# Two blocks with expert layers on one core: new heads for the expert stages, and the third down matrix loaded in mixer 2

## The reference

```
g_idx = argmax(group logits);  e_logits = expert logits of that group
top_v, top_i = top_k(e_logits, 2);  gate = softmax(top_v) * softmax(group logits)[g_idx]
out = sum over the token's 2 experts:  gate * ((silu(x @ w1[e]) * (x @ w3[e])) @ w2[e])
```

## Time and profile before

| | |
|---|---|
| median of 3 runs | 1572.54 us (1571.43 to 1575.5) |
| profiled execution, span from first to last instruction | 1574.9 us (no time outside the span is shown) |
| mean granted clock of TensorE | 0.939 of full speed |
| busy: PE, DVE, ACT, POOL | 1353.3, 689.2, 247.8, 80.0 us |
| moved by DMA | 528.20 MB, mean 335 GB/s |
| first expert stage begins | 167.5 us |
| second expert stage begins | 1124.2 us |

### The profile page before, as it was taken

One profiled execution on the slowest core, in us unless ns is written; L12 is line 12 of the kernel. 1 busy time (PEld: TensorE's weight loads), 2 busy tenths in 40 slices (PEclk: granted clock), 3 DMA queues, 4 the chain that ended last, 5 costly groups with the idle time before them and its releaser, 6 DMA issues. The chain is left out here.

```text
span 1574.9 us, 27743 instructions
## 1 busy us (share of the span) xinstructions
PE 1353.3 (86%) x11912; PEld 876.2 (56%) x11912; DVE 689.2 (44%) x1844; ACT 247.8 (16%) x505; POOL 80.0 (5%) x125
## 2 busy tenths in 40 slices
PE   9999998997978789899999999999896676666665
PEld 8655554553455566588767748886453343333332
DVE  4634664322223343427687536652562332332333
ACT  2322330110001111233223113230200000000000
POOL 2401000000000000030000200100000000000000
PEclk9999999999988999999999999999998878887887
DMA  9965899999999999877522454476999999999996
GB/s 336 270 232 191 335 426 429 424 425 427 427 430 425 426 425 427 352 251 280 200 93 106 148 174 160 165 284 257 381 393 429 429 430 429 431 430 430 430 427 252
DMA packets 94023, 528.20 MB, mean 335 GB/s; under 512 B 8282, under 2 KB 10610, under 8 KB 67684
## 3 DMA queue, kind: packets, MB, share of 16 engines
q1 hardware_dynamic: 88792, 521.30, 81.8%
q0 software_dynamic: 2624, 5.32, 1.4%
q10 hardware_dynamic: 2508, 0.17, 0.1%
HBM read 525.70 MB, written 1.07 MB: 334 GB/s over the span
## 5 line engine op out<-in xcount | busy, mean ns | idle before, releaser
L1568 PE MATMUL ps<-weight_ring,e_xT 128*32 128x256 f32 x3456 | 247.8, 449 | 131.4 <-DMA weight_ring<-in_w_up_dram 89.2
L1568 PEld LDWEIGHTS ps<-weight_ring,e_xT 128*32 128x32 f32 x3456 | 137.0, 128 | 237.6 <-issue 192.7
L1848 DVE TENSOR_TENSOR e_g<-e_act_g,ps 128x128 f32<-128x128 f32 x64 | 24.8, 388 | 263.5 <-ACT e_act_g L1655 262.3
L1846 DVE TENSOR_TENSOR e_act_g<-e_act_g,ps 128x128 f32<-128x128 f32 x32 | 9.2, 286 | 236.2 <-ACT e_act_g L1655 236.2
L1655 ACT ACTIVATE e_act_g<-ps 128x128 f32<-128x128 f32 x64 | 17.8, 278 | 565.5 <-PE ps L1568 558.3
L1568 PE MATMUL ps<-expert_set,e_xT 128*32 128x256 f32 x640 | 51.3, 491 | 42.5 <-DMA expert_set<-in_w_up_dram 42.5
L1598 PE MATMUL ps<-weight_ring,e_gT 128*32 128x256 f32 x1344 | 82.6, 387 | 4.2 <-DVE e_gT L1852 2.0
L2369 PE MATMUL ps<-expert_set,weight_ring 128*128 128x256 f32 x384 | 84.2, 379 | 0.0
L2369 PEld LDWEIGHTS ps<-expert_set,weight_ring 128*128 128x128 f32 x384 | 73.0, 190 | 9.9
L1532 PE MATMUL ps<-e_y,e_routing 32*128 32x256 f32 x1024 | 74.3, 404 | 2.1 <-DVE e_y L1880 1.5
L1524 PE MATMUL ps<-e_n,e_Gt 128*32 128x256 f32 x1056 | 70.9, 385 | 3.8 <-DVE e_Gt L1795 2.0
(11 more groups left out here) (614 smaller groups left out, 1945.4 us busy)
## 6 DMA issues: line engine op xcount, KB each, us to landing
weight_ring<-in_expert_w_dram SPq DMA_DIRECT2D x80, 2048.0 KB, 23.0
weight_ring<-in_w_in_dram SPq DMA_DIRECT2D x26, 2048.0 KB, 9.6
weight_ring<-in_w_down_dram SPq DMA_DIRECT2D x20, 2048.0 KB, 38.8
weight_ring<-in_w_gate_dram SPq DMA_DIRECT2D x19, 2048.0 KB, 32.9
weight_ring<-in_w_up_dram SPq DMA_DIRECT2D x19, 2048.0 KB, 37.4
weight_ring<-in_w_ada_dram SPq DMA_DIRECT2D x12, 2048.0 KB, 12.6
expert_set<-in_w_gate_dram SPq DMA_DIRECT2D x10, 2048.0 KB, 33.4
expert_set<-in_w_up_dram SPq DMA_DIRECT2D x10, 2048.0 KB, 37.9
```

Source lines behind the costliest of these rows:

```text
L1568: mm = pe.matmul(ps[32 * j:32 * j + 32, 4, 0:256].rearrange("p (w f) -> p w f", w=2), xT[:, k, :], w13[:, :, k, j * P:(j + 1) * P], start= ...
L1848: dve.tensor_tensor(g[:], spread(act_g[:]), spread(ps[:, 4, P:2 * P]), ALU.mult).then_inc(s_g, 1)
```

## The change

In `moe`:

- Expert 0 gets a direct mask: a token takes it if group 0 holds the group maximum and the expert's logit reaches the second highest of the group's eight. Two small position matmuls (`first_positions`) and a one-hot come from that alone. The full choice follows, while PE gathers expert 0 and does its up.
- The full position matmuls (`positions`) stand in the middle of expert 0's up, the one-hots of experts 1 and 2 come straight from positions and choices, and slots, gates and `wide` are worked out in DVE's part of expert 0.
- PE transposes `wide` in expert 1, behind its gather and in front of its combine (then behind expert 0's down). In stage 1 the residual stands behind expert 1's up (then expert 0's).
- The counts of `keep_busy` are others, and in stage 2 the residual is split around the first steps.
- In stage 2 a down is now queued behind an earlier expert's pair (`DOWN_AFTER`), and `load_down(2)` is no longer in the head.

In `mixer2`: the transposed `h` goes where `yT` was, the router's buffers (`spare`) to the end of `FT`, the squares' junk to `misc`; the third down of stage 2 is loaded behind piece 22 (the first of branch b).

The order of the downs:

```diff
-        DOWN_AFTER.update((i, i) for i in range(11 if SETS == 2 else 5, STATIC))
+        DOWN_AFTER.update(((i, i) for i in range(11, STATIC)) if SETS == 2 else
+                          ((i, {3: 6, 5: 5}.get(i, i + 1)) for i in range(3, STATIC - 1) if i != 4))
...
-            for i in (2, 4) if last else (3,):
+            for i in (4,) if last else (3,):
                 load_down(i)
```

PE, the head (`positions` holds the four matmuls of L1516 to L1519, `first_positions` two for expert 0):

```diff
+            def first_positions():
+                pe.wait_ge(s_hot0, 1)
+                pe.wait_ge(s_iota, 1)
+                pe.matmul(pos0_ps, tri[:], hot0, start=True, stop=False, skip_group_check=True)
+                pe.matmul(pos0_ps[:, 1:2], c.ones[:], hot0[:, 0:1], start=False, stop=True, skip_group_check=True).then_inc(s_pos0, 1)
+            def positions():
+                pe.wait_ge(s_hot, 1)
...
             if x is not None:
                 x.pe_transposes(pe)
-                keep_busy(c, pe, 7, 11)
+                keep_busy(c, pe, 7, 2)
             else:
-                residual()
-                keep_busy(c, pe, 7, 4)
+                residual((0, 1))
+            first_positions()
+            if x is not None:
+                keep_busy(c, pe, 7, 6)
+            else:
+                residual((2,))
             pe.wait_ge(s_n, 2)
             pe.wait_ge(s_Gt, 1)
             gather()
-            keep_busy(c, pe, 7, 4)
+            if x is not None:
+                keep_busy(c, pe, 7, 8)
+            else:
+                residual((3,))
+                keep_busy(c, pe, 7, 3)
```

PE, `expert(i)`, behind the first half of the up and behind its end:

```diff
                     if known and i == 0 and k == KD // 2 - 1:
                         mm.then_inc(s_uph, 1)
+                        positions()
...
-                if first:
-                    if x is not None:
-                        x.pe_taken(pe)
-                        residual()
-                elif x is not None and known:
+                if x is not None and second:
+                    x.pe_taken(pe)
+                    residual()
+                if x is not None and known and not first:
                     x.pe_early(pe, i)
                 pe.wait_ge(s_Gt, i + 2)
                 pe.wait_ge(s_y, i + 1)
                 gather()
+                if second:
+                    pe.wait_ge(s_slot, 1)
+                    for v in range(8):
+                        mm = pe.transpose(ps[:, 6 + v // 4, (v % 4) * P:(v % 4 + 1) * P], wide[:, v, :], c.ident[:])
+                    mm.then_inc(s_rows, 1)
                 if not first:
-                    pe.wait_ge(s_Gw, i + 1)
+                    pe.wait_ge(s_Gw, i)
                     combine()
```

DVE, the head; left out are the group index and mask and the best two, as before but with `take_x(0)` among them, the copy of the positions, the one-hot of expert 1 and the block counts:

```diff
             link(dve.tensor_reduce(gm[:], gl, AX_X, ALU.max))
+            for tt in range(TT):
+                ins = dve.max(top8[:, tt, :], el[:, tt, 0:EPG])
+            link(ins)
+            link(dve.tensor_tensor(slot[:, 1, :], el[:, :, 0], top8[:, :, 1], ALU.is_ge))
+            link(dve.tensor_tensor(hot0, gl[:, :, 0], gm[:], ALU.is_ge))
+            dve.tensor_tensor(hot0, hot0, slot[:, 1, :], ALU.mult).then_inc(s_hot0, 1)
...
+            dve.wait_ge(s_pos0, 1)
+            link(dve.tensor_copy(pos0, pos0_ps))
+            for tt in range(TT):
+                ins = dve.tensor_scalar(Gt[:, tt, :], ie[:], pos0[:, tt:tt + 1], hot0[:, tt:tt + 1], ALU.is_equal, ALU.mult)
+            ins.then_inc(s_Gt, 1)
```

DVE, expert 0 behind its product, `take_x(1)` and the gather of block 1; then `GwT` as before:

```diff
                 dve.wait_ge(s_gather, i + 2)
+                begin = isinstance(i, int) and i == 0
+                if begin:
+                    early_one_hot(2)
+                    slots_and_gates()
+                    gated_y()
                     rows()
+                    step(VO - 4, dve.tensor_scalar(slot[:], slot[:], -2.0 * SLOTS, None, ALU.add))
```

`mixer2`, the buffers, SP's loads and ACT's squares:

```diff
-        hT, spare = nT, nTp[:].rearrange("p k n -> p (k n)")
+        hT, spare = yT, FT[:, 4128:4128 + 2048]
...
-        junk = FT[:, 4128:4128 + 2048]
+        junk = [misc[:, 512 * g:512 * g + 512] for g in range(3)] + [FT[:, 2080:2592]]
...
             for p in M2_ISSUE:
                 sp.wait_ge(*used(M2_BEFORE[p]))
                 m2_load(c, sp, t, p)
+                if p == 22:
+                    sp.wait_ge(s_fl, 16)
+                    load_one(c, sp, c.s_e2, 2, 2, W, third=c.three)
...
             for g in range(3):
                 act.wait_ge(s_h, g + 1)
+                if g == 2:
+                    act.wait_ge(s_arow, 48)
                 squares(g)
```

More of the change, by code:

```diff
@@ L1344, in moe @@
         slot = sb("slot", [P, 2, TT])
+        hot0, pos0 = slot[:, 0, :], gate[:, 1, :]
         over = etmp
@@ L1500, in _, with residual @@
         def _(pe):
-            def residual():
-                for m in range(4):
+            def residual(ms=range(4)):
+                for m in ms:
                     mm = pe.matmul(ps[:, m, :].rearrange("p (t n) -> p t n", t=TT), c.ident[:], h[:, :, m * 256:(m + 1) * 256],
                               start=True, stop=False, skip_group_check=True)
-                mm.then_inc(s_comb, 1)
-            if x is not None:
-                x.pe_transposes(pe)
-                keep_busy(c, pe, 7, 11)
-            else:
-                residual()
-                keep_busy(c, pe, 7, 4)
[L1514 to L1519, removed]
+                if ms[-1] == 3:
+                    mm.then_inc(s_comb, 1)
+            def first_positions():
[5 more added lines that the diff above has]
+                pe.wait_ge(s_hot, 1)
+                pe.matmul(pos_ps, tri[:], both[:].rearrange("p t e -> p (t e)"), start=True, stop=False, skip_group_check=True)
+                pe.matmul(pos_ps[:, NE:2 * NE], c.ones[:], both[:, 0, :], start=False, stop=True, skip_group_check=True).then_inc(s_pos, 1)
+                pe.matmul(tot_ps, c.ones[:], both[:, 0, :], start=True, stop=False, skip_group_check=True)
+                pe.matmul(tot_ps, c.ones[:], both[:, 1, :], start=False, stop=True, skip_group_check=True).then_inc(s_tot, 1)
             def gather():
@@ L1600, in expert @@
                 mm.then_inc(s_down, 1)
[L1601 to L1605, removed]
                 if x is not None and second:
@@ L1749, in _ @@
             link(ins)
+            dve.wait_ge(s_Gt, 1)
+            dve.tensor_tensor(gate[:, 0, :], top8[:, :, 1], top8[:, :, 0], ALU.subtract).then_inc(s_vd, 1)
             below(etmp, em, lambda tt: top8[:, tt, 0:1], NE)
             link(below(pos, em, lambda tt: top8[:, tt, 1:2], NE))
+            take_x(0)
             link(dve.tensor_reduce(topi[:], etmp[:], AX_X, ALU.min))
@@ L1798, in _ @@
-            dve.wait_ge(s_ve, 1)
-            link(dve.tensor_scalar(gate[:, 0, :], gate[:, 1, :], 1.0, None, ALU.add))
-            link(dve.tensor_tensor(gate[:, 0, :], gate[:, 0, :], gprob[:], ALU.mult))
-            link(dve.reciprocal(gate[:, 0, :], gate[:, 0, :]))
-            link(dve.tensor_tensor(gate[:, 1, :], gate[:, 0, :], gate[:, 1, :], ALU.mult))
-            if last:
-                dve.wait_ge(s_comb, 1)
-                dve.wait_ge(s_n, 2)
-            for v in range(8):
-                src = (slot, gate)[v // 4][:, (v // 2) % 2, v % 2:v % 2 + 1]
-                ins = dve.tensor_copy(wide[:, v, :], src.to_broadcast([P, P]))
@@ L1877, in expert @@
                     block_table()
-                if mod is not None:
-                    dve.wait_ge(s_down, i + 1)
-                    dve.tensor_tensor(y[:], ps[:, 5, 0:256], gate_m[:], ALU.mult).then_inc(s_y, 1)
+                if not begin:
+                    gated_y()
             if mod is not None:
@@ L2088, in _ @@
         def _(sp):
+            W = [t[x] for x in ("w_gate_2", "w_up_2", "w_down_2")]
             for p in M2_ISSUE:
@@ L2601, in squares @@
                 at = 2 * tile + half
-                act.activation(junk[:, g * 512:g * 512 + 512], h[:, tile, half * 512:half * 512 + 512], ACT.Square,
+                act.activation(junk[g], h[:, tile, half * 512:half * 512 + 512], ACT.Square,
                                accum_out=stat[:, 0, at:at + 1]).then_inc(s_hsq, 1)
```

104 lines of the change are left out of this document (54 added, 50 removed).

## The result

The changed kernel takes 1580.07 us (median of 8 runs, 1578.08 to 1582.44); beside it, on the same chip, the kernel before took 1575.5 (8 runs, 1571.43 to 1576.65). The ratio is 1.0034 with a 95% interval of 1.0024 to 1.0044: some 5.4 us slower (0.0034 x 1575.5). The forecast was 1571.8 with 1577.3 as its upper end; it stood on 1572.54, the median of three runs of the kernel before, where the eight give 1575.5.

The account below looks back on a forecast made before the run. SP's weight stream was taken to bound the expert stages and PE's chain mixer 2. First head +3.5, mixer 2's tail +1.7 and second head -5.9 gave -0.7 us on 1572.54: 1571.8, range 1566.3 to 1577.3.

Parts of the forecast that it names:

- What bounds the kernel: SP's weight stream bounds both expert stages, so time lost at a head stays; in mixer 2 PE's chain counts.
- A: First expert stage's head: the chain through expert 1 delays weight loads, costing +3.5 us.
- E4: Load of expert 4's gate and up pair; first-stage issue forecast at 209.8, second-stage at 1142.4.
- E5: Load of expert 5's gate and up pair; first-stage issue forecast at 224.1, second-stage at 1156.3.
- clock rival: PE's pause before combine 1 lowers its clock in both heads: first head +6.9, second -2.8, total 1578.3; chance 0.17.
- The two rows: Old-profile idle windows for judging the clock: 259 to 262, then clock 0.57; 1537 to 1541, clock kept at 1.00.
- the forecast pause of 3.75 us: First head: PE idles in front of combine 1, from 192.8 to 196.55, while DVE copies rows and builds weights.
- B: Mixer 2's tail: the early third down delays the last modulation piece by 4.9 us, costing +1.7 us.
- C: Second expert stage's head: earlier up 0 and one down fewer there, gaining 5.9 us.
- What I costed at nothing: Mixer 2's moved transposed h, router buffers and squares' junk, and the third square's added wait: 0 us.
- The sum and its range: +3.5 + 1.7 - 5.9 = -0.7 us, giving 1571.8; range 1566.3 to 1577.3 to hold 8 in 10.
- its base: Starting time 1572.54 us, the old kernel's median, taken though the profiled span was 1574.9.

Follow-up runs that it names:

- experiment 3: Changed kernel with the first expert stage as in the kernel before; 1575.79 us, ratio 1.0005 to the kernel before.
- experiment 4: Changed kernel with the old first expert stage and the third down issued behind mixer 2's last modulation piece; 1570.40 us, ratio 0.9972 to the kernel before.
- experiment 5: Kernel before with only the changed first expert stage put in; 1580.93 us, ratio 1.0038 to the kernel before.
- experiment 11: Changed kernel, first stage's residual behind the transposes, third down loaded at the second stage's head, none in mixer 2; 1574.80 us, ratio 0.9997.
- experiment 2: Changed kernel with the third down issued behind mixer 2's last modulation piece instead of in front; 1575.96 us, ratio 0.9997 to the kernel before.
- experiment 7: Changed kernel with the first stage's residual behind the transposes, in front of combine 1; 1572.93 us, ratio 0.9990 to the kernel before.
- 1: Changed kernel with 14 filler matmuls in the first stage's pause in front of combine 1; 1577.00 us, ratio 1.0011 to the kernel before.
- experiment 8: Changed kernel with the edits of experiment 2 and experiment 7 together; 1570.91 us, ratio 0.9967 to the kernel before.
- experiments 9: Kernel of experiment 8 with 12 filler matmuls in the second head's pause in front of combine 1; 1569.77 us, ratio 0.9960 to the kernel before.
- 12: Experiment 8 plus 12 fillers in the second head's pause and two behind the first stage's gate matmuls; 1568.64 us, ratio 0.9962 to the kernel before.

## Why the prediction was wrong, point by point

**What bounds the kernel: right.** Late issues at a head were not made up over 400 us of stream (6.2 us late at 373, 5.65 at 694), and mixer 2's wait of PE came through in full (2.99 us of wait, mixer 2 longer by 3.06).

**A, the chain through expert 1: right, but for its clock.** Gather 0, up 0, residual, combine 1 and the pause came within 0.25 us. With the pause filled, E4, E5 and the loss (2.6 us in the middle of the stage) come near the forecast's 209.8, 224.1 and +3.5. The step that failed is the one that let this chain run at full clock: I gave the lower clock to a rival at 0.17. It took place, and A was 5.65 to 6.55 in three profiles and some 6.0 by the ratio, near that rival's +6.9. The two rows from which I let it be decided were read too narrowly. Timeline of PE in the kernel before, from 1537 on:

```profile
1540.24 1.93 PE L1568 MATMUL ps<-weight_ring,e_xT 128*32 128x256 f32 x32 [3.03 <-DMA weight_ring<-in_w_up_dram]
...
1550.07 3.64 PE L1568 MATMUL ps<-weight_ring,e_xT 128*32 128x256 f32 x32 [3.07 <-DMA weight_ring<-in_w_up_dram]
```

The row that kept its clock is one wait of 3.03 us with full speed behind it; 10 us later a wait of 3.07 us has half speed behind it (the granted clock is 0.53 from 1549 to 1553), and the row at 259 is a wait of 4.00 us. So two of these three waits lost the clock, and the forecast pause of 3.75 us was longer than the one that kept it. A chance of 0.17 was too low for that.

The Trainium skill (TensorE: Matmul & The Clock Gate, section HAM oscillation) says that waits between bursts send the array back to its lower clock. By that rule the rival was the forecast; here the trace agrees (0.50 from 196 to 200, behind the pause of 3.76 us), and I was wrong to let one row outweigh it.

**B, the early down: mechanism right, size too small, and its clock left out.** The piece came 6.4 us later, not 4.9: SP's own issue of the down (0.6) and 2.1 MB at the 372 GB/s of that stretch (5.6), where I had used 427. PE's wait of 2.99 us follows from that, and B is 3.06 in the profile. I had no term for the clock in this wait. Experiments 3 and 4 put B at some 5 us in the ratios; that what exceeds the wait is the clock is seen in two of four profiles (4.4 and 7.45 us), but its share in the median is not settled.

```profile
1029.30:1048.67 19.37, 19.37 (x92) 17.03 (x91) 4.86 (x18) 3.66 (x9) 0.29 (x1) 1.00 1.02 372
```

**C, the second head: mechanism right, size too large.** -5.9 was forecast and some -4.4 measured by the ratio of experiment 4 (interval -2.8 to -6.0). Up 0 is 3.0 us sooner after the stage's first issue (2.7 forecast), and E4 as forecast. That the profiles give -6.4 is in part luck: the kernel before had lost its own clock in this head (0.58 from 1139 to 1143), so its down 0 was slow and E4 went out 24.5 us behind the stage's first issue. In experiment 5 the same old stage kept its clock, E4 came after 23.2 us, and beside that profile C is -3.1. The two downs 0, before and in experiment 5:

```profile
1141.21 2.81 PE L1598 MATMUL ps<-weight_ring,e_gT 128*32 128x256 f32 x32 [0.60 <-issue]
...
1147.12 1.93 PE L2255 MATMUL ps<-weight_ring,e_gT 128*32 128x256 f32 x32 [0.62 <-DVE e_gT L2509]
```

The forecast took E4 at 1148.70 from that one trace as the old stage's fixed time. And one thing that I had not seen was needed for the gain: the down that left the queue no longer stands in front of the gate rows (experiment 11).

**What I costed at nothing**: the moved buffers, rightly (experiment 2).

**The sum and its range.** The sign was lost in the clock behind one pause (3.6 us) and in a price of B that was too low by 1.4 us in its wait and by more in the ratio; C gained less than forecast on top. The clock rival's own sum, +5.8, is near the measured +5.4, but its terms are not: it had B at 1.7 (some 5 measured) and C at -2.8 (some -4.4), errors that partly cancel. The number had a second fault, in its base. I saw the span 2.4 us above the median of three runs, with no time shown around it, and went by the median. In all later profiles 1.7 or 1.8 us lie outside the span, so by that the profiled execution took some 1576.6 us; and the median of eight runs is 3.0 us above that of the three. On 1575.5 the same sum gives 1574.8 and the same range ends at 1580.3: 3.0 of the 8.3 us between 1571.8 and 1580.07 are the base and no mechanism.

## What to carry to other kernels

A pause of PE can have two prices: itself, and what runs at half clock behind it; the second can be the larger (2.95 us of wait and 4.5 more in experiment 3). When work is moved, look for what is left in its old place to keep PE busy, and put it between the producer and the waiter: the residual between the transposes and the combine removed 3.4 us of pause without adding work. A load put in front of another on the same queue delayed that one by its whole transfer at the rate of that stretch (6.4 us for 2.1 MB), and the 32 KB loads of the gate rows landed 11.4 us after their issue behind two downs, 7.0 behind one. And before a row of a trace is taken as the fixed time of the old kernel, look whether its clock was full there, and at a second profile of the same code.

## What the runs showed of the hardware that I had not expected

Sixteen such single waits in the profiles of the changed kernels (2.8 to 3.8 us in front of combine 1 or of the gated rows) can be compared. In front of combine 1 of the first stage (3.8 us) the clock fell in 3 of 3 without fillers; of the second (3.1 us) it was low in 9 of 9, though in experiment 3 it had fallen before that wait; in mixer 2, with 2.8 to 3.0 us, it fell in 2 of 4. With fillers it fell in 0 of 5. The same wait of mixer 2 thus made it 3.0 and 3.1 us longer in the two profiles that kept the clock (7 and the changed kernel), 4.4 and 7.45 in the two that lost it (1 and 3). That this is one source of the spread from run to run is likely, but no run shows it.

The clock can also fall without a long wait. In experiment 8 PE's longest idle stretch from 192 to 204 was 0.62 us, yet its clock was 0.71 from 204 to 208, and E4 went out at 207.29; experiments 9 and 11 did the same (0.77 and 0.82), while experiment 7 ran the same order there at 1.00, and so did the five profiles with the old first stage, which have that wait of 0.6 us too. It matters: the reordered first stage begins mixer 2 at 685.9 in the two profiles that kept the clock (7, 12) and at 688.15 to 689.96 in the three that lost it; the kernel before begins it at 688.76.

```profile
200.00:204.00 4.00, 3.93 (x40) 1.80 (x44) 0.84 (x2) 1.08 (x3) 0.00 (x0) 0.87 0.98 418
204.00:208.00 4.00, 4.00 (x56) 1.97 (x48) 1.08 (x6) 0.69 (x2) 0.00 (x0) 0.71 0.91 381
```

What tells these executions apart stays open.
